# Encoder trunk with grouped experts: expert results read back in eight transfers, all first choices ahead of all second choices

## The chip, the cores and the metric

The kernel runs on one core of a Trainium2 chip. The metric is the device time of one execution in microseconds, the median over several runs. A core has TensorE (PE in the profile), VectorE (DVE), ScalarE (ACT), GpSimd (POOL) and SyncE (SP), which follow their own instruction streams and meet at semaphores, and sixteen DMA engines.

## The reference

Two groups of 256 tokens (512 in all) of width 1024 pass through two encoder layers with shared weights. In float32, a layer is attention in two forms, a gated merge, and then a mixture of experts, in which every token goes to its best two of sixteen experts:

```python
h2 = rms_norm(x, norm_ffn) * (1 + scale2) + shift2
x = x + gate2 * grouped_moe(h2, ...)      # w[t, j]: weight of the token's j-th choice, j = 0, 1
# grouped_moe: out[t] = w[t, 0] * expert_(e[t,0])(h2[t]) + w[t, 1] * expert_(e[t,1])(h2[t])
...
return rms_norm(x, final_norm)            # after layer 2
```

(The reference adds all sixteen experts with a gate that is zero for fourteen of them; the comment gives the sum that is left.) The change lies between the experts' outputs and the `x + gate2 * ...` of both layers.

## The kernel before, in words

All tokens are on the core, in four blocks of 128 (TT = 4). The residual stream is kept transposed in the tensor xT (features on partitions), the experts' rows are not: a tile of 128 token rows is gathered for an expert, goes through its gate, up and down products, and its output rows are scattered by GpSimd to a DRAM tensor y_dram (`y_by_choice`, 1024 rows). Row t of its first half is the output of the first choice of token t, row t of its second half that of the second choice. Tiles are worked in pairs (par 0 and 1); a loop over the pairs, whose length is read from a plan at run time, loads each expert's weights through six ring slots.

When all scatters are stored, the rows are read back to SBUF, into the tensor zone: got[0] for the first choices (4 blocks of 1024 numbers per partition) and got[1] for the second. This is done by load_rows_back (line 675), which SyncE runs at two places.

At the boundary between the layers SyncE has issued the loads of the next layer's first four modulation weight blocks. It then waits for the last scatter (y_stored), issues the readback (line 680), and behind it the loads of the next blocks of the input projection (`qa`, `kva`, `qb`, `kb`; line 673). All go through SyncE's one DMA queue. ScalarE, after copying four modulation rows, does weigh_first (line 1318): for each block it waits for got_rows[t] and scales the first choice by its weight (line 1322). VectorE does combine (line 1851): for each block it waits for ScalarE's count got_weighed and adds the weighted second choice (line 1855). TensorE transposes each block (line 876) to its banks. VectorE then makes the low part of the first weight group (low_part, line 1770), for which ScalarE must have made the high part from the landed block `qa` (line 1316), and only after it adds the gated rows to xT (line 1847). Squares and the norm of the next layer follow.

At the end the order is different. While the rows are on their way, TensorE makes rows of the gates (line 1224) and puts xT, turned back to token rows, into eight banks (line 1232). ScalarE goes through the blocks (lines 1679 to 1686): it weighs block t (line 1681), and from t = 2 on it does the squares and root of block t - 2 (tok_rms, lines 1670 to 1676) after that, so the fourth weighing stands behind the root of block 0. VectorE does gated_sum for blocks 0, 1 and 2: the sum (line 2392) and the product with the gate row (line 2396). Then it scales block 0 by its inverse root (lines 2401 and 2406), does gated_sum for block 3, and scales blocks 1, 2 and 3. TensorE adds each gated block to its banks (line 1238), and SyncE stores each scaled block (line 756).

Before the change a transfer carries both choices of one block (1024 KB, one semaphore got_rows[t]), so whoever waits for the first choice has the second too, and VectorE needs no wait of its own for a DMA.

Of the kernel before, what the change touches and what calls it, by code (L numbers as in the profile page):

```python
# [29 lines left out]
P = 128  # L30
# [4 lines left out]
TOK = SEQ * GROUPS  # L35
TT = TOK // P
DEPTH = 2
# [321 lines left out]
def build_trunk(nc, t_in, y_prompt, y_sample):  # L359
# [7 lines left out]
    with ctx:  # L367
# [3 lines left out]
        def sem(name):  # L371
            return ctx.enter_context(nc.semaphore(name))
# [3 lines left out]
        y_dram = nc.dram_tensor("y_by_choice", (2 * TOK, D), F32, kind="Internal").ap()  # L376
# [24 lines left out]
        def part(at, n):  # L401
            return z[:, at:at + n]
# [31 lines left out]
        got_both = part(0, 8192).rearrange("p (j t d) -> p j t d", j=2, t=TT)  # L434
        got = (part(0, 4096).rearrange("p (t d) -> p t d", t=TT), part(4096, 4096).rearrange("p (t d) -> p t d", t=TT))
# [103 lines left out]
        h2_out = sem("h2_out")  # L539
        index_now = sem("index_now")  # L540
        got_rows = [sem(f"got_rows{t}") for t in range(TT)]
        arrived = sem("arrived")
        go = sem("go")
        planned = sem("planned")
# [106 lines left out]
        def _(sp):  # L651
# [23 lines left out]
            def load_rows_back(pairs, layer):  # L675
                for par in range(2):
                    sp.wait_ge(y_stored[par], pairs * 16 + 16)
                nc.sync.sem_inc(sp_passed, 1)
                for t in range(TT):
                    sp.dma_start(got_both[:, :, t, :],  # L680
                                 y_dram.rearrange("(j t p) d -> p j t d", j=2, p=P)[:, :, t, :])\
                      .then_inc(got_rows[t], 16)

            for t in range(TT):
                x_in = t_in[("x_prompt", "x_sample")[t // 2]]
# [2 lines left out]
            for layer in range(DEPTH):  # L688
# [4 lines left out]
                for b in BLOCKS:  # L693
                    if not TURN[b]:
                        par = 0 if SLOT[b] in EXPERT_SLOTS[0] else 1
                        left = LAST_PARTS[par][EXPERT_SLOTS[par].index(SLOT[b])]
                        sp.wait_ge(part_used, before * 12 + PARTS_BEFORE - left)
                        nc.sync.sem_inc(sp_passed, 1)
                    if b == "qa" and layer:
                        load_rows_back(before, layer)  # L700
                    if TURN[b]:

                        sp.wait_ge(used[SLOT[b]], layer * SLOT_BLOCKS[SLOT[b]] + TURN[b])
                    load(layer, b)
# [44 lines left out]
            nc.sync.sem_inc(sp_passed, 1)  # L749
            sp.dma_start(norm_row, t_in["final_norm"].partition_broadcast(P)).then_inc(in_norm_row, 16)  # L750
            load_rows_back(pairs, DEPTH)

            for t in range(TT):
# [938 lines left out]
        def _(dve):  # L1692
# [73 lines left out]
            def low_part(n):  # L1766

                b, c = W_GROUPS[n]
                dve.wait_ge(S["w_hi_ready"], n + 1)
                v.tensor_tensor(group_view(w_lo[SLOT[b]], b, c), group_view(ring[SLOT[b]], b, c),  # L1770
                                w_hi[:, n % W_BUFS, :, :].bitcast(F32), ALU.subtract).then_inc(S["w_lo_ready"], 1)
# [70 lines left out]
            def add_gated(use, key, j, which):  # L1842

                ps = wait_full(dve, use, key)
                for g in range(GROUPS):
                    x = xT[:, j, g * SEQ:(g + 1) * SEQ]
                    ins = v.scalar_tensor_tensor(x, ps[:, g * SEQ:(g + 1) * SEQ],
                                                 mod[:, 3 * KC * which + 2 * KC + j, g:g + 1], x, ALU.mult, ALU.add)
                freed(ins, use, key)

            def combine(own, use, layer, nth):

                for t in range(TT):
                    dve.wait_ge(S["got_weighed"], nth * TT + t + 1)
                    v.scalar_tensor_tensor(got[0][:, t, :], got[1][:, t, :], gw[:, 1, t:t + 1], got[0][:, t, :],
                                           ALU.mult, ALU.add).then_inc(S["mix_ready"], 1)
                low_part(0)
                for c in range(KC):
                    add_gated(use, ("back", c), c, 1)
                for n in range(1, W_BUFS):  # L1860
                    low_part(n)

            for layer in range(DEPTH):
# [32 lines left out]
                if layer:  # L1896
                    combine(own, use, layer, 0)
                    norm_rstd(own, use, 0)
# [490 lines left out]
            def gated_sum(t):  # L2389

                dve.wait_ge(S["got_weighed"], TT + t + 1)
                own.step(v.scalar_tensor_tensor(got[0][:, t, :], got[1][:, t, :], gw[:, 1, t:t + 1], got[0][:, t, :],
                                                ALU.mult, ALU.add))
                own.last()
                dve.wait_ge(gate_rows_ready, 2 * GROUPS)
                v.tensor_tensor(got[0][:, t, :], got[0][:, t, :], gate_rows[:, t // 2, :], ALU.mult).then_inc(gated, 1)
# [13 lines left out]
            for t in range(3):  # L2410
                gated_sum(t)
            scaled_rows(0)
            gated_sum(3)
            for t in range(1, TT):
                scaled_rows(t)
# [110 lines left out]
```

## Time and profile before

| What | Value |
|---|---|
| Median of 3 runs | 1549.5 us (1547.37 to 1552.57) |
| Profiled execution, its own time | 1550.57 us |
| Its span in the profile | 1548.7 us |
| TensorE busy | 1432.5 us, 92% |
| VectorE busy | 1006.8 us, 65% |
| ScalarE busy | 865.1 us, 56% |
| GpSimd busy | 122.4 us, 8% |
| DMA, mean over the span | 220 GB/s |

The span is the time from the first to the last record. Busy times of different engines lie beside each other and don't add up to it. A DMA's landing is seen from when its semaphore released someone. The readback takes place twice, from 765 us and from 1523 us of the span.

### The profile page before, as it was taken

How to read it: one execution, taken by the hardware profiler on the slowest of the kernel's cores; microseconds unless marked ns; L12 is line 12 of the kernel's file. 1: busy time of each engine (PE TensorE's matmuls, PEld its weight loads, DVE VectorE, ACT ScalarE, POOL GpSimd, SP SyncE). 2: the span in 40 equal slices, each digit the busy share in tenths (PEclk: the TensorE clock that was granted, in tenths of full speed). 3: DMA queues.
4: the chain of work that ended last, by engine and by line, in shares of the span. 5: the costliest groups of instructions: out<-in, count | busy, mean ns of one | idle time of the engine just before them, and what ended most of it. 6: DMA issues, size and time to landing. Idle time of an engine off the chain costs nothing. (4 is left out here: it accounts for less than half of the span.)

```text
span 1548.7 us, 19269 instructions
## 1 busy us (share of the span) xinstructions
PE 1432.5 (92%) x6810; PEld 1088.1 (70%) x6810; DVE 1006.8 (65%) x1256; ACT 865.1 (56%) x1232; POOL 122.4 (8%) x143
## 2 busy tenths in 40 slices
PE   5799989999889999999859999899997999999997
PEld 2677558887667777777537765688774877777775
DVE  1565685325388888888363929733255888888874
ACT  4632595323257777777354228822225577777764
POOL 1000000000021111122000000000000121111110
PEclk8899999999999999999969999999998999999998
DMA  9622761113359999999763138211145599999944
GB/s 325 233 101 104 271 219 55 55 55 109 127 187 353 364 374 357 363 354 361 263 220 109 55 118 321 106 55 55 57 161 194 204 368 369 364 367 361 360 177 167
DMA packets 148368, 341.49 MB, mean 220 GB/s; under 512 B 8351, under 2 KB 10545, under 8 KB 148176
## 3 DMA queue, kind: packets, MB, share of 16 engines
q1 hardware_dynamic: 136880, 317.20, 56.3%
q0 software_dynamic: 10704, 22.57, 4.1%
q10 hardware_dynamic: 720, 0.87, 0.2%
q8 instruction: 39, 0.64, 0.2%
q14 instruction: 25, 0.20, 0.0%
HBM read 333.08 MB, written 24.12 MB: 231 GB/s over the span
## 5 line engine op out<-in xcount | busy, mean ns | idle before, releaser
L778 PE MATMUL bank<-x_hi,w_lo 128*128 128x512 f32 x608 | 244.1, 402 | 19.7 <-DVE w_lo L1770 7.3
L779 PE MATMUL bank<-x_lo,w_hi 128*128 128x512 f32 x608 | 238.8, 393 | 0.0
L780 PE MATMUL bank<-x_hi,w_hi 128*128 128x512 f32 x608 | 238.8, 393 | 0.0
L2278 DVE TENSOR_TENSOR w_lo<-ring,x_lo 128x2048 fp32r<-128x2048 f32 x92 | 210.4, 2289 | 29.0 <-ACT x_lo L1586 28.6
L1586 ACT CAST zone_r<-ring 128x2048 fp32r<-128x2048 f32 x92 | 176.0, 1913 | 28.5 <-PE bank L1155 16.1
L1586 ACT CAST x_lo<-ring 128x2048 fp32r<-128x2048 f32 x92 | 176.1, 1918 | 26.3 <-PE bank L1170 14.6
L1153 PE MATMUL bank<-w_lo,zone_r 128*128 128x512 f32 x384 | 156.0, 406 | 0.0
L1770 DVE TENSOR_TENSOR w_lo<-ring,w_hi 128x1024 fp32r<-128x1024 f32 x84 | 102.2, 1221 | 81.6 <-ACT w_hi L1316 80.9
L778 PEld LDWEIGHTS bank<-x_hi,w_lo 128*128 128x128 f32 x608 | 115.3, 190 | 51.6 <-issue 23.0
L779 PEld LDWEIGHTS bank<-x_lo,w_hi 128*128 128x128 f32 x608 | 115.3, 190 | 26.3 <-issue 2.4
L780 PEld LDWEIGHTS bank<-x_hi,w_hi 128*128 128x128 f32 x608 | 115.1, 189 | 24.6
L1316 ACT CAST w_hi<-ring 128x1024 fp32r<-128x1024 f32 x84 | 87.3, 1046 | 26.7 <-PE bank L780 13.1
L1155 PE MATMUL bank<-zone_r 128*128 128x512 f32 x256 | 101.3, 396 | 0.0
L1154 PE MATMUL bank<-zone_r 128*128 128x512 f32 x256 | 100.9, 394 | 0.0
L1521 ACT ACTIVATE zone<-bank 128x512 f32<-128x512 f32 x32 | 19.1, 598 | 136.1 <-PE bank L780 136.0
L1154 PE MATMUL bank<-x_lo,zone_r 128*128 128x512 f32 x240 | 95.1, 396 | 0.0
L1155 PE MATMUL bank<-x_lo,zone_r 128*128 128x512 f32 x240 | 95.0, 396 | 0.0
L2278 DVE TENSOR_TENSOR w_lo<-ring,zone_r 128x2048 fp32r<-128x2048 f32 x32 | 73.4, 2292 | 21.7 <-ACT zone_r L1586 21.4
L1153 PEld LDWEIGHTS bank<-w_lo,zone_r 128*128 128x128 f32 x384 | 72.3, 188 | 15.5 <-issue 0.2
L2278 DVE TENSOR_TENSOR w_hi<-ring,zone_r 128x2048 fp32r<-128x2048 f32 x32 | 73.4, 2292 | 6.2 <-ACT zone_r L1586 6.0
L2443 POOL DMA_DIRECT2D rows_by_token<-zone x8 | 4.4, 548 | 826.6 <-ACT zone L1569 825.8
L2446 POOL DMA_INDIRECT zone<-rows_by_token,row_now x28 | 53.7, 1917 | 201.3 <-DMA y_by_choice<-zone,row_now 196.1
(316 smaller groups left out, 2766.4 us busy)
## 6 DMA issues: line engine op xcount, KB each, us to landing
ring<-in_w_gate SPq DMA_DIRECT2D x32, 2048.0 KB, 13.7
ring<-in_w_up SPq DMA_DIRECT2D x32, 2048.0 KB, 14.9
ring<-in_w_down SPq DMA_DIRECT2D x32, 2048.0 KB, 9.7
ring<-in_w_ada SPq DMA_DIRECT2D x24, 2048.0 KB, 13.5
ring<-in_w_in SPq DMA_DIRECT2D x16, 2048.0 KB, 7.9
ring<-in_w_out SPq DMA_DIRECT2D x4, 2048.0 KB, 7.7
zone<-y_by_choice SPq DMA_DIRECT2D x8, 1024.0 KB, 8.0
ring<-in_w_branch_a SPq DMA_DIRECT2D x2, 2048.0 KB, 8.3
```

The costliest lines, as they stand in the source:

```text
L778: mm(out, lo, x_first, start=start, stop=False)
L779: mm(out, hi, x_second, start=False, stop=False)
L780: return mm(out, hi, x_first, start=False, stop=stop)
L1153: mm(out, xg_hi[:, par, c, :], wv[:, c, :], start=(c == 0), stop=False)
L1154: mm(out, xg_lo[:, par, c, :], hi[:, k, :], start=False, stop=False)
L1155: ins = mm(out, xg_hi[:, par, c, :], hi[:, k, :], start=False, stop=(c == KC - 1))
L1316: nc.scalar.copy(w_hi[:, n % W_BUFS, :, :], group_view(ring[SLOT[b]], b, c)).then_inc(S["w_hi_ready"], 1)
L1521: af(gates[:, n % 2, :], ps[:, :], ACT.Sigmoid).then_inc(S["gate_ready"], 1)
L1586: nc.scalar.copy(part_hi[buf], ring[EXPERT_SLOTS[par][k]][:, h * 2048:(h + 1) * 2048])\
L1770: v.tensor_tensor(group_view(w_lo[SLOT[b]], b, c), group_view(ring[SLOT[b]], b, c), w_hi[:, n % W_BUFS, :, :].bitcast(F32), ALU.subtract). ...
L2278: v.tensor_tensor(w_low[EXPERT_SLOTS[par][k]][:, cols], ring[EXPERT_SLOTS[par][k]][:, cols], part_hi[buf].bitcast(F32), ALU.subtract)\
L2446: pool.indirect_dma_start(xg[:, par, :], None, h2_dram, bass.IndirectOffsetOnAxis(ap=index, axis=0), bounds_check=TOK - 1, oob_is_err=Fals ...
```

## The change

Each of the four transfers of both choices is replaced by two of 512 KB: SyncE issues the first choices of blocks 0 to 3, then the second choices of blocks 0 to 3. The second choices have four semaphores of their own, got_second, and VectorE waits for them ahead of each sum, at both places.

```diff
--- before.py
+++ after.py
@@ -539,6 +539,7 @@
         h2_out = sem("h2_out")
         index_now = sem("index_now")
         got_rows = [sem(f"got_rows{t}") for t in range(TT)]
+        got_second = [sem(f"got_second{t}") for t in range(TT)]
         arrived = sem("arrived")
         go = sem("go")
         planned = sem("planned")
@@ -677,9 +678,10 @@
                     sp.wait_ge(y_stored[par], pairs * 16 + 16)
                 nc.sync.sem_inc(sp_passed, 1)
                 for t in range(TT):
-                    sp.dma_start(got_both[:, :, t, :],
-                                 y_dram.rearrange("(j t p) d -> p j t d", j=2, p=P)[:, :, t, :])\
-                      .then_inc(got_rows[t], 16)
+                    sp.dma_start(got[0][:, t, :], y_dram[t * P:(t + 1) * P, :]).then_inc(got_rows[t], 16)
+                for t in range(TT):
+                    sp.dma_start(got[1][:, t, :], y_dram[TOK + t * P:TOK + (t + 1) * P, :])\
+                      .then_inc(got_second[t], 16)
 
             for t in range(TT):
                 x_in = t_in[("x_prompt", "x_sample")[t // 2]]
@@ -1852,6 +1854,7 @@
 
                 for t in range(TT):
                     dve.wait_ge(S["got_weighed"], nth * TT + t + 1)
+                    dve.wait_ge(got_second[t], layer * 16)
                     v.scalar_tensor_tensor(got[0][:, t, :], got[1][:, t, :], gw[:, 1, t:t + 1], got[0][:, t, :],
                                            ALU.mult, ALU.add).then_inc(S["mix_ready"], 1)
                 low_part(0)
@@ -2389,6 +2392,7 @@
             def gated_sum(t):
 
                 dve.wait_ge(S["got_weighed"], TT + t + 1)
+                dve.wait_ge(got_second[t], DEPTH * 16)
                 own.step(v.scalar_tensor_tensor(got[0][:, t, :], got[1][:, t, :], gw[:, 1, t:t + 1], got[0][:, t, :],
                                                 ALU.mult, ALU.add))
                 own.last()
```

## Rows read from the trace of the kernel before

**Rows 1.** The page's list of DMA issues (out<-in, engine, operation, count, KB each, median us to landing)

```profile
zone<-y_by_choice SPq DMA_DIRECT2D x8, 1024.0 KB, 8.0
```

**Rows 2.** Source lines 680 (read back) and 756 (store): duration in ns, landing in us

```profile
L680 SPq DMA_DIRECT2D zone<-y_by_choice x8: 372/470/783, 765.4 to 1524.5; - x8
...
L756 SPq DMA_DIRECT2D out<-zone x4: 332/341/351, 1538.2 to 1545.7; - x4
...
DMA to landing us min/median/max: 2.6/2.6/2.7
```

**Rows 3.** Chain of waits, the last 50 us (start us, us, what)

```profile
1523.01 4.78 DMA zone<-y_by_choice
1527.82 1.16 ACT zone L1681
...
1529.08 1.29 DVE zone L2392
1530.40 1.22 DVE zone L2396
1531.62 1.23 DVE zone L2392
...
1539.41 1.24 DVE zone L2396
...
1540.69 2.00 PE bank L1238 x4
```

**Rows 4.** Timeline of the end (start us, us, engine, line, operation; in brackets the idle time before, its releaser)

```profile
1523.01 2.13 SPq L680 DMA_DIRECT2D zone<-y_by_choice  x4
...
1530.37 1.15 ACT L1681 ACTIVATE zone<-zone,gw 128x1024 f32<-128x1024 f32 x1 [1.41 <-DMA zone<-y_by_choice]
...
1531.68 7.11 PE L1238 MATMUL bank<-zone,const 128*128 128x512 f32 x12 [3.19 <-DVE zone L2396]
...
1532.93 1.15 ACT L1681 ACTIVATE zone<-zone,gw 128x1024 f32<-128x1024 f32 x1 [1.41 <-DMA zone<-y_by_choice]
...
1535.98 0.29 ACT L1676 ACTIVATE four<-four 128x1 f32<-128x1 f32 x1
...
1536.58 0.15 DVE L2401 RECIPROCAL four<-four 128x1 f32<-128x1 f32 x1
```

**Rows 5.** Windows (us, each engine's busy us, granted clock PEclk, DMA share, GB/s)

```profile
1509.00:1515.00 6.00, 5.82 (x14) 4.56 (x15) 3.12 (x16) 0.00 (x0) 0.00 (x0) 0.50 0.00 0
...
1529.00:1531.00 2.00, 0.00 (x0) 0.00 (x0) 1.89 (x2) 0.63 (x1) 0.00 (x0) 1.00 1.01 410
1533.00:1534.00 1.00, 1.00 (x3) 0.32 (x1) 1.00 (x1) 1.00 (x2) 0.00 (x0) 0.50 1.01 406
1536.00:1537.00 1.00, 1.00 (x4) 0.47 (x3) 0.96 (x3) 1.00 (x2) 0.00 (x0) 1.00 0.00 0
```

**Rows 6.** Timeline of the boundary between the layers, columns as in rows 4

```profile
765.43 2.23 SPq L680 DMA_DIRECT2D zone<-y_by_choice  x4
...
767.71 16.80 SPq L673 DMA_DIRECT2D ring<-in_w_in  x4
...
773.48 2.48 DVE L1855 SCALAR_TENSOR_TENSOR zone<-zone,gw 128x1024 f32<-128x1024 f32 x2 [0.16 <-DVE mul L1830]
...
779.27 1.15 ACT L1322 ACTIVATE zone<-zone,gw 128x1024 f32<-128x1024 f32 x1 [1.42 <-DMA zone<-y_by_choice]
780.45 1.29 DVE L1855 SCALAR_TENSOR_TENSOR zone<-zone,gw 128x1024 f32<-128x1024 f32 x1 [1.28 <-ACT zone L1322]
781.79 1.97 PE L876 MATMUL bank<-const,zone 128*128 128x128 f32 x8 [1.47 <-DVE zone L1855]
784.78 3.88 ACT L1316 CAST w_hi<-ring 128x1024 fp32r<-128x1024 f32 x4 [4.36 <-DMA ring<-in_w_in]
785.86 1.22 DVE L1770 TENSOR_TENSOR w_lo<-ring,w_hi 128x1024 fp32r<-128x1024 f32 x1 [4.12 <-ACT w_hi L1316]
787.00 6.35 DVE L1847 SCALAR_TENSOR_TENSOR xT<-bank,mod,xT 128x256 f32<-128x256 f32 x16
```

## The prediction, made before the changed kernel was run

> **What bounds the kernel now.** I looked first for the two places where the results are read back, then asked of each what ended its last wait. The page's list of DMA issues [rows 1] shows the eight 1024 KB transfers that the change touches: four at the start of the second layer, four at the end. Everything else stays as it is, so only these two stretches, about 20 us each, can give or lose time.
>
> *The end.* The chain of waits [rows 3] runs: last scatter lands, SyncE issues at 1523.01, the first transfer lands 4.78 us later, ScalarE weighs the first choice from 1527.82, VectorE adds the second choice from 1529.08. From there to 1540.65 the chain is VectorE alone: sum, multiply, sum, multiply, without a gap. Then come the last block's products on TensorE (1540.69), its squares and root on ScalarE, and the last scaling and store. So VectorE's start sets the end, one for one, as long as nothing starves it later.
>
> *The layer boundary.* The timeline [rows 6] shows the same work there, but the four sums end at 780.45 + 1.29 = 781.74, the last transposes at 781.79 + 1.97 = 783.76, and then all engines wait for a weight block: ScalarE's cast at 784.78 was idle for 4.36 us until ring<-in_w_in landed. VectorE's part of that block (785.86) stands ahead of its gated additions (787.00) in program order. The weight block ends the last wait, and the readback has 787.00 - 783.76 = 3.2 us of slack.
>
> **The change part by part.**
>
> *Bytes and their order.* The bytes are the same, 4 MB per place; only the order differs. Before, the transfers land at intervals of one block: ScalarE's waits end at 1527.82, 1530.37 and 1532.93 [rows 3, 4], 2.55 us apart. The windows show 410 GB/s during them [rows 5], and 1.05 MB at 0.41 MB a microsecond is 2.56 us, so they follow one another in order with no gap. A half of the size then takes 1.275 us. The second choice of block 0 is the fifth of eight, two and a half old transfers from the front instead of one. It lands 1.5 x 2.55 = 3.83 us after the old first: 1527.79 + 3.83 = 1531.62.
>
> *ScalarE's weighing.* The weighing of 1.15 us now lies beside the transfers: first choices land near 1526.5, 1527.8, 1529.1 and 1530.3, so block 0 is weighed by 1527.7, and blocks 1 and 2 by 1530.3. ScalarE's fourth weighing stays behind the root of block 0 in program order, and moves with it.
>
> *VectorE's start at the end.* Before 1529.08; after 1531.62 and the 0.05 us that such a handover takes: 1531.67. That is 2.59 us later.
>
> *VectorE afterwards.* The chain has 2.54 us a block (1529.08 to 1531.62 [rows 3]); second choices land every 1.275 us, so blocks 1 to 3 have theirs in time (at 1532.9, 1534.2 and 1535.5, wanted at 1534.2, 1536.8 and 1540.7). VectorE runs without a gap as before, only 2.59 us later. Nothing is handed back: the last block's transfer is not what the old chain waits for.
>
> *The added waits.* Eight waits on VectorE (four a place), whose semaphores are filled for all but the first. Queued behind each are the sum, the multiply, and for TensorE the block's products. The trace has no such wait alone; a sum and the multiply after it, which already has two waits between them, stand 0.03 us apart (1529.08 + 1.29 to 1530.40 [rows 3]). Bounds 0 to 0.05 us each, four at each place; I take 0, nearest to that gap, and keep 0.2 us for the range.
>
> *The issues.* SyncE issues eight in place of four. The old ones take 0.37 to 0.78 us (median 0.47) each, and a 512 KB store takes 0.34 [rows 2]. Eight cost 8 x 0.34 = 2.7 to 8 x 0.53 = 4.2 us against 2.13 [rows 4]. At the end the fifth leaves by 1523.01 + 5 x 0.53 = 1525.7, and its bytes are not wanted before 1530.3: hidden. The first may start moving up to 0.2 us sooner, because its issue is shorter; I take 0 and keep -0.2. At the boundary the queued issues behind them are the weight blocks: the first would leave 2.1 us later than 767.71, near 769.8, while the queue has readback bytes until about 779: hidden. With that cover gone it would cost those 2.1 us.
>
> *The boundary.* The weight block follows the same 4 MB in the same queue, so it lands when it did: 0. First choices are weighed ahead of the sums. The last sum no longer waits for a weighing and can start when the last transfer lands (779.27, where ScalarE's wait for it ends, in place of 780.45), so the transposes end about 1.2 us sooner and wait longer for the same weight block. If that block were not the limit, those 1.2 us would be a gain; VectorE's first sum (773.48) now waits for the fifth half, to 779.25 - 3 x 1.275 = 775.4, and that too stays in the slack, since the sums follow at 1.3 us each and the last starts at 779.3.
>
> *TensorE's clock.* At the end TensorE sits idle for 3.19 us before block 0's products start at 1531.68 [rows 4]; this becomes 5.8 us. The granted clock is 0.50 (the lower level, 1.2 GHz) in the slice at 1533 and 1.00 (2.4 GHz) in that at 1536 [rows 5], so the lower level came within 1.3 us of the restart and was gone 4.3 us after it. After the longer idle time it may already hold at the restart: what ran at the full level, 1.3 us at most, would take as long again. Behind it the root of block 0 comes at 1535.98 + 0.29 = 1536.27 and VectorE asks for it at 1536.58 [rows 4], 0.3 us of cover. Bounds 0 and 1.3 - 0.3 = 1.0 us; I take 0, because the level had fallen early in block 0 as it is, and keep the 1.0. The stretch 1509 to 1515 held 0.50 for 6 us [rows 5]; even that would be over at 1534.3 + 6 = 1540.3, before the last block's products at 1543.3.
>
> *A price for size.* With 410 GB/s and 2.55 us spacing the rows show no fixed cost between transfers of 1 MB. A lone 512 KB store takes 2.6 us from issue to landing [rows 2] against 1.275 of movement, so up to 1.3 us of fixed time per transfer exists and is either hidden by the next or not. The trace has no queue of 512 KB transfers alone. Bounds 0 and 1.3 us each; I take 0, nearest to the spacing row, as the next transfer's bytes are already queued.
>
> The Trainium skill (DMA: Bandwidth & Descriptors, "Anatomy of one DMA" and "Measured") gives each transfer a fixed 2.0 us and advises at least 1 MiB per transfer. The trace agrees for a transfer alone (4.78 less 2.55 is 2.2 us) and not for one in a queue (2.55 us apart); by the page's formula paid in full, each half-size transfer would take 3.2 us, an estimate from that page, and the change would be clearly slower, as in the second rival.
>
> **The sum.** End +2.59, boundary 0, other terms 0: +2.6 us. Against the profiled execution (1550.57 us, span 1548.7) that is 1553.2. This execution stood 1.07 us above the median of 1549.5; the prediction is for medians: 1549.5 + 2.6 = 1552.1 us. That is 0.17% slower, less than the 0.3% (4.6 us) that a measurement of this kernel can tell from no change.
>
> **The rivals.**
>
> *The last landing counts (faster).* If both places are bound by when block 3 is complete, weighing drops out behind it and each gives 1.2 us: 1549.5 - 2.4 = 1547.1. For it: at the boundary ScalarE waited 1.42 us for the last transfer [rows 6]. Against it: the weight block comes later still [rows 6], and VectorE has no gap at the end [rows 3]. Only mixtures of it are likely. Chance 0.06.
>
> *Gaps between the smaller transfers (clearly slower).* Place: the SyncE queue, both places. Each of eight transfers leaves a gap g that its successor doesn't cover. The end pays four gaps before the fifth lands, and the weight block at the boundary stands behind eight and pays 8g (the four before show no gap). Total 2.6 + 4g + 8g. It passes 4.6 us from g = 0.17 us. With g = 0.3 it is 1549.5 + 2.6 + 3.6 = 1555.7; with the full 1.3 it is 1549.5 + 2.6 + 15.6 = 1567.7. Chance 0.12, mostly near the low end.
>
> *Nothing moves.* If the second choices land early, since the sixteen engines drain the queue unevenly, or the first bytes start sooner, VectorE starts where it did: 1549.5. Against it: the landings are evenly spaced. Chance 0.08.
>
> **How the numbers follow.** The forecast has 0.74, with its own range from 2.59 - 0.2 to 2.59 + 0.2 + 1.0, which is 1551.9 to 1553.3, and about 1 us either way for the scatter of a median (the runs shown span 5.2 us): 1551 to 1554. Range for 8 in 10: from 1549.0, which takes in "nothing moves", to 1555.0, which takes in gaps up to 0.24 us. Within 0.3%: most of the forecast, all of "nothing moves" and most of the first rival, 0.77; slower 0.18 (the gaps, and the forecast with unlucky scatter); faster 0.05.
>
> **What would show it.** In the changed kernel: first choices land 1.3 us apart; ScalarE weighs three blocks before VectorE's first sum; that sum follows a DMA, not ScalarE, at about 8.7 us after the first issue (6.07 before); VectorE then has no gap until the last products. At the boundary the cast still waits for the weight block; its distance from the first issue is 784.78 - 765.43 = 19.35 us before [rows 6]. If it grows by more than 0.3 us, the smaller transfers cost something. If VectorE's first sum at the end comes within 7 us of the first issue, the order argument is wrong.

## The result, and the profile after

The changed kernel takes 1555.21 us in the median of 20 runs (1550.61 to 1559.43), the kernel before 1549.26 us in 20 runs (1546.56 to 1556.28). The ratio is 1.0037, with a 95% interval of 1.0025 to 1.0048: about 5.7 us slower (3.9 to 7.4), where 2.6 us were forecast. That is 0.2 us above the upper end of the range, 1555.0, and on the slower side of the 0.3% line, though the interval takes in 0.3%. The ratios of this document leave out two slow executions, of 2383 us (pairs) and 2850 us (before).

| | Before | After |
|---|---|---|
| Profiled execution, its own time | 1550.57 us | 1553.39 us |
| Span | 1548.7 us | 1551.3 us |
| First readback issue at the end, to the end of the span | 1548.7 - 1523.01 = 25.7 us | 1551.3 - 1520.02 = 31.3 us |
| First readback issue at the end, to VectorE's first sum | 6.07 us | 1530.13 - 1520.02 = 10.11 us |
| First readback issue at the boundary, to the cast of the weight block | 19.35 us | 783.25 - 763.77 = 19.48 us |

The two spans alone would mislead: this execution of the changed kernel reached the last readback 3 us earlier than that of before, so the span grew by 2.6 us only. The profiles of all kernels here reach it anywhere from 1519.8 to 1523.0 us. The last stretch shows the loss, 5.6 us, and that agrees with the ratio. A single profile of this stretch can be a microsecond off, though: the kernel boundary_only below, whose end is that of before, has 26.9 us.

The timeline of the end of the changed kernel answers to [rows 3] and [rows 4] (start us, us, engine, line, operation, count; in brackets the idle time before and its releaser):

```profile
1520.02 1.88 SPq L681 DMA_DIRECT2D zone<-y_by_choice  x4
1521.94 1.94 SPq L683 DMA_DIRECT2D zone<-y_by_choice  x4
1523.24 1.15 ACT L1683 ACTIVATE zone<-zone,gw 128x1024 f32<-128x1024 f32 x1 [2.67 <-DMA zone<-y_by_choice]
1525.15 1.15 ACT L1683 ACTIVATE zone<-zone,gw 128x1024 f32<-128x1024 f32 x1 [0.76 <-DMA zone<-y_by_choice]
1527.43 1.15 ACT L1683 ACTIVATE zone<-zone,gw 128x1024 f32<-128x1024 f32 x1 [1.14 <-DMA zone<-y_by_choice]
1530.13 1.28 DVE L2396 SCALAR_TENSOR_TENSOR zone<-zone,gw 128x1024 f32<-128x1024 f32 x1 [20.79 <-DMA zone<-y_by_choice]
1531.45 1.22 DVE L2400 TENSOR_TENSOR zone<-zone,ring 128x1024 f32<-128x1024 f32 x1
1532.59 1.28 DVE L2396 SCALAR_TENSOR_TENSOR zone<-zone,gw 128x1024 f32<-128x1024 f32 x1
1532.72 6.96 PE L1240 MATMUL bank<-zone,const 128*128 128x512 f32 x12 [7.23 <-DVE zone L2400]
...
1538.12 1.41 DVE L2410 SCALAR_TENSOR_TENSOR zone<-bank,four,ring 128x512 f32<-128x512 f32 x2 [0.30 <-DVE four L2405]
...
1539.45 1.27 DVE L2396 SCALAR_TENSOR_TENSOR zone<-zone,gw 128x1024 f32<-128x1024 f32 x1
...
1542.04 3.18 PE L1240 MATMUL bank<-zone,const 128*128 128x512 f32 x4 [2.35 <-DVE zone L2400]
...
1546.83 1.41 DVE L2410 SCALAR_TENSOR_TENSOR zone<-bank,four,ring 128x512 f32<-128x512 f32 x2
```

The 5.6 us come apart here. VectorE's first sum now waits for a DMA, not for ScalarE, and its distance from the first issue has grown by 4.04 us. The fourth sum follows the first by 9.32 us (1538.10 - 1529.08 = 9.02 before): 0.3 us. From the last block's products to the last scaling pass 1546.83 - 1542.04 = 4.79 us, against 1544.28 - 1540.69 = 3.59 before, since the products took 3.18 us and not 1.98: 1.2 us. The rest is 0.05.

The rate of the transfers while they run, for before and then for the changed kernel (slices of 0.35 us from the first issue):

```profile
GB/s 23 0 35 152 117 421 328 433 374 456 421 421 386 456 421 421 386 456 421 421 386 433 433 398 410 386 410 421 421 410 398 386 445 117 0 0 0 0 0 0
```

```profile
GB/s 23 0 59 199 211 398 386 386 421 386 351 199 140 269 304 328 339 375 363 316 351 421 410 421 398 445 421 410 410 445 421 410 410 410 351 176 164 82 0 0
```

Before holds about 415 GB/s from its sixth slice to the end. After falls to 140 GB/s some 4 us in and is back near 415 only at 7.4 us. That is the hole of which the experiments below speak. In these 14 us no queue but SyncE's moves more than one packet (0.01 MB), so it is not another queue's traffic that takes the engines away. The first choices show the hole too: ScalarE's waits for them end 3.2, 5.1 and 7.4 us after the first issue, 1.9 and 2.3 us apart, where 1.3 us apart was forecast.

The boundary, which answers to [rows 6]:

```profile
763.77 1.78 SPq L681 DMA_DIRECT2D zone<-y_by_choice  x4
765.59 1.98 SPq L683 DMA_DIRECT2D zone<-y_by_choice  x4
...
773.98 5.13 DVE L1858 SCALAR_TENSOR_TENSOR zone<-zone,gw 128x1024 f32<-128x1024 f32 x4 [2.32 <-DMA zone<-y_by_choice]
775.31 5.05 PE L878 MATMUL bank<-const,zone 128*128 128x128 f32 x32 [4.44 <-DVE zone L1858]
783.25 3.88 ACT L1318 CAST w_hi<-ring 128x1024 fp32r<-128x1024 f32 x4 [8.76 <-DMA ring<-in_w_in]
```

The transposes end at 775.31 + 5.05 = 780.4, 16.6 us after the first issue (18.3 before), and the cast still waits for the weight block, now with 8.76 us of idle time before it in place of 4.36. Everything that moved lies in that idle time.

### The profile page after: what moved, and what is told of

It reads as the page before. It is cut to its first block and busy times, and to the rows that moved or that the text cites. A ratio compares the mean times of both kernels' runs of the same rounds, so it can differ in the third digit from the quotient of the medians.

```text
span 1551.3 us, 19284 instructions
## 1 busy us (share of the span) xinstructions
PE 1430.7 (92%) x6810; PEld 1087.4 (70%) x6810; DVE 1007.0 (65%) x1256; ACT 865.1 (56%) x1232; POOL 119.7 (8%) x143
## 5 line engine op out<-in xcount | busy, mean ns | idle before, releaser
L2096 DVE TENSOR_TENSOR zone<-bank,zone 128x512 f32<-128x512 f32 x16 | 11.1, 692 | 86.8 <-PE bank L782 86.8
```

## The experiments

Theory at the start: the loss is at the end, and has three parts: the order of the bytes, a hole in the queue that comes with half-size transfers, and TensorE's clock. Each ratio is against executions of the kernel before that were measured beside it. "Above before" is this ratio times 1550 us; the difference of the plain medians departs from it by up to 1.2 us. "First sum" and "last stretch" are in us from the first readback issue of the end, and like the last column they come from one profiled execution each.

| Kernel | Ratio, 95% interval | First sum | Last stretch | Boundary: issue to cast |
|---|---|---|---|---|
| before | 1 | 6.07 | 25.7 | 19.35 |
| changed | 1.0037, 1.0025 to 1.0048 | 10.11 | 31.3 | 19.48 |
| changed_again | 1.0038, 1.0021 to 1.0056 | 10.16 | 30.4 | 20.87 |
| end_only | 1.0023, 1.0009 to 1.0038 | 9.32 | 29.3 | 19.37 |
| boundary_only | 1.0004, 0.9993 to 1.0014 | 6.34 | 26.9 | 20.27 |
| pairs | 1.0007, 0.9995 to 1.0020 | 5.00 | 26.0 | 19.87 |
| megabyte | 1.0035, 1.0022 to 1.0048 | 10.43 | 31.6 | 19.54 |
| one_early | 1.0015, 1.0003 to 1.0026 | 5.79 | 28.3 | 19.69 |
| mixed | 1.0022, 1.0009 to 1.0035 | 9.04 | 29.7 | 19.42 |
| fill | 1.0030, 1.0018 to 1.0043 | 10.18 | 30.5 | 19.48 |
| before_fill | 1.0002, 0.9988 to 1.0016 | 6.07 | 25.7 | 19.33 |
| pairs_fill | 0.9995, 0.9982 to 1.0008 | 5.69 | 27.5 | 19.99 |

**end_only.** The new transfers and VectorE's new wait at the end only:

```diff
-                for t in range(TT):
-                    sp.dma_start(got_both[:, :, t, :], ...).then_inc(got_rows[t], 16)
+                if layer == DEPTH:
+                    ...  # the eight transfers of the changed kernel
+                else:
+                    ...  # the four of before
```

> Eight transfers, first choices first, at the end alone; at the layer boundary the four old transfers of both choices. In the profiles of before and after, the stretch from the first readback issue of the end to the end of the span went from 1548.7 - 1523.01 = 25.7 us to 1551.3 - 1520.02 = 31.3 us, 5.6 us more, and the boundary's stretch from first issue to the cast of the weight block from 19.35 to 19.48 us. Theory (the end holds the whole loss): this kernel is as slow as the changed one, 5 to 6 us above before, ratio 1.0032 to 1.0038, and its last stretch takes 30 to 31.5 us. Rival (gaps between smaller transfers at both places): about 2 to 4 us above before, since the boundary's share is missing.

Measured: 1.0023, 3.5 us above before (1.4 to 5.9); last stretch 29.3 us, just under the 30 to 31.5 forecast. The time lies in the rival's range of 2 to 4 us and not in the theory's 5 to 6, but its interval reaches into both. So the end holds most of the loss; that it holds all of it is not shown. In this profile the hole was small (its lowest slice has 269 GB/s, first sum at 9.32 us, not 10.1).

**boundary_only.** The same with the condition the other way round, and VectorE's new wait only there:

```diff
-                if layer == DEPTH:
+                if layer < DEPTH:
```

> The eight transfers at the layer boundary alone; at the end the four old ones. Theory (the boundary waits for the weight block anyway): the time of before within 1 us, ratio 0.9993 to 1.0007; the cast of the first weight block starts 19.3 to 19.6 us after the first readback issue. Rival (gaps): 2 to 4 us slower, the cast more than 20.5 us after the first issue.

Measured: 1.0004, no loss that can be told (-1.1 to 2.2 us). But the cast came 20.27 us after the first issue, 0.9 us later, between the two expectations. In the seven profiles with eight half-size transfers at the boundary the distance is 19.48, 20.87, 20.27, 19.87, 19.69, 19.48 and 19.99, mean 19.95; in those with four transfers it is 19.33 to 19.37 (19.54 in megabyte). So the weight block lands 0.6 us later on average, and the sums play no part in it. The dip differs between executions: in slices of 0.5 us, the lowest rate between 4 and 5 us after the first issue is 172 GB/s in boundary_only, 254 in changed_again, 295 in changed and 328 in fill, with the cast at 20.27, 20.87, 19.48 and 19.48 us. Whether the 0.6 us reach the end is not shown: from the first issue at the boundary to the first issue at the end, the profiles with the four old transfers at the boundary take 755.7 to 757.6 us, those with eight 754.8 to 757.6.

**pairs.** All eight transfers, in the order of blocks:

```diff
                 for t in range(TT):
                     sp.dma_start(got[0][:, t, :], y_dram[t * P:(t + 1) * P, :]).then_inc(got_rows[t], 16)
-                for t in range(TT):
                     sp.dma_start(got[1][:, t, :], y_dram[TOK + t * P:TOK + (t + 1) * P, :])\
```

> The same eight 512 KB transfers, semaphores and waits as the changed kernel at both places, but in the order first choice of block 0, second choice of block 0, first of block 1, and so on. Theory A (the order alone makes the loss): VectorE's first sum comes 1.2 us sooner than before (6.07 us after the first issue before, 4.9 here), since the weighing lies beside the second transfer, and the kernel is 0 to 1.2 us faster than before. Theory B (half-size transfers also leave holes in the queue; the profile after shows 184 GB/s in the slice 4 us after the first issue, and the second choice of block 0 landed 10.0 us after it and not 8.6): the first sum comes at 5 to 6.5 us, and later sums wait for transfers; within 1.5 us of before, on either side.

Measured: 1.0007, 1.1 us above before, which can't be told from equal (-0.8 to 3.1 us). With the same sizes, number and waits as the changed kernel most of the 5.7 us are gone, and the two intervals lie apart; so the order makes most of the loss. What theory B says of the holes also shows:

```profile
1527.95 1.28 DVE L2395 SCALAR_TENSOR_TENSOR zone<-zone,gw 128x1024 f32<-128x1024 f32 x1 [14.70 <-DMA zone<-y_by_choice]
1529.27 1.23 DVE L2399 TENSOR_TENSOR zone<-zone,ring 128x1024 f32<-128x1024 f32 x1
1530.24 1.15 ACT L1682 ACTIVATE zone<-zone,gw 128x1024 f32<-128x1024 f32 x1 [2.81 <-DMA zone<-y_by_choice]
...
1531.69 1.28 DVE L2395 SCALAR_TENSOR_TENSOR zone<-zone,gw 128x1024 f32<-128x1024 f32 x1 [1.19 <-DMA zone<-y_by_choice]
```

These are VectorE's first two sums, with the issue at 1522.95. The first comes at 5.00 us, 1.07 earlier than before. The second waits 1.19 us for a transfer and comes at 8.74 us (8.55 in the timeline of before): what hiding the weighing won was lost again while transfers ran behind their even pace, down to 234 GB/s in one slice.

**megabyte.** Choice by choice in four transfers of 1024 KB:

```diff
+                for t in range(0, TT, 2):
+                    sp.dma_start(got[0][:, t:t + 2, :], y_dram[t * P:(t + 2) * P, :].rearrange("(t p) d -> p t d", p=P))\
+                      .then_inc(got_rows[t], 16)
+                ...  # the same for got[1]; waits on got_rows and got_second of block t // 2 * 2
```

> Choice by choice, but in four transfers of 1024 KB: first choices of blocks 0 and 1, first choices of blocks 2 and 3, then the second choices likewise. The second choice of block 0 is complete with the third transfer. If only bytes and order count: it lands 4.78 + 2 x 2.55 = 9.9 us after the first issue, as late as the 10.0 us of the changed kernel, and the kernel is as slow as the changed one, 5 to 6 us above before. If reading whole choices (rows that lie one after another) is itself slower than reading both choices alternately, it lands at 11 us or later and the kernel is 7 us or more above before. If the holes belong to the half size, the landings are evenly 2.5 to 2.6 us apart, as in before.

Measured: 1.0035 in five executions, 5.4 us above before and as slow as the changed kernel, with no hole. Its rates from the first issue:

```profile
GB/s 23 0 59 70 12 152 363 421 398 410 456 410 410 410 456 410 410 410 456 410 410 386 433 421 421 398 375 433 433 410 398 386 410 421 129 0 0 0 0 0
```

The first landing ends ScalarE's wait 0.4 us later than in before (after 5.19 us, not 4.81), and the third transfer is complete after 10.4 us in place of 9.9. That it is as slow as the changed kernel is a balance of two things: here 3 MB must land ahead of the first sum and there is no hole, in the changed kernel 2.5 MB and the hole. So order by choice alone costs about 5 us when the transfers are this large, the clock's share included (the last block's products took 3.26 us here). Reading whole choices runs at 410 GB/s like before, no slower in itself.

**one_early.** The second choice of block 0 moved from fifth place to second:

```diff
+                for j, t in [(0, 0), (1, 0), (0, 1), (0, 2), (0, 3), (1, 1), (1, 2), (1, 3)]:
+                    sp.dma_start(got[j][:, t, :], ...).then_inc((got_rows, got_second)[j][t], 16)
```

> The changed kernel with one transfer moved, at both places: the second choice of block 0 goes second instead of fifth; all else, sizes and waits, as changed. Theory (VectorE's last wait for a second choice sets the end): VectorE sums block 0 at 5.0 us after the first issue and then waits for the second choice of block 1, now the sixth transfer, which lands at 4.78 - 1.28 + 5 x 1.275 = 9.9 us, or up to 1.4 us later with a hole in the queue; in before that block's sum started at 8.6. So 1.3 to 2.7 us above before from the transfers, with TensorE's clock 1.3 to 4 us, against 5.6 for the changed kernel. Rival (eight transfers cost their time by number and size, not by order): as slow as the changed kernel, 5 us or more above before.

Measured: 1.0015, 2.3 us above before (0.5 to 4.0). The issue is at 1520.28:

```profile
1526.07 1.28 DVE L2394 SCALAR_TENSOR_TENSOR zone<-zone,gw 128x1024 f32<-128x1024 f32 x1 [15.25 <-DMA zone<-y_by_choice]
...
1531.49 1.28 DVE L2394 SCALAR_TENSOR_TENSOR zone<-zone,gw 128x1024 f32<-128x1024 f32 x1 [2.88 <-DMA zone<-y_by_choice]
```

VectorE waits 2.88 us for block 1, whose sum comes at 11.21 us, 2.7 later than before; the last stretch is 2.6 us longer too (28.3). The loss follows the last second choice that VectorE waits for: one transfer moved, and more than half of it is gone.

**fill.** TensorE turns three blocks of xT back twice at the end; the first result is overwritten:

```diff
+            for t in range(3):
+                for half in range(2):
+                    ps = take(final_use, ("x_tok", t, half))
+                    for q in range(4):
+                        mm(ps[:, q * P:(q + 1) * P], xT[:, 4 * half + q, t * P:(t + 1) * P], K("ident"),
+                           start=(q == 0), stop=(q == 3))
```

> The changed kernel with TensorE given 24 more groups of identity products at the end (three of the four blocks of xT are turned back twice, the first result overwritten), so that it sits idle for about 1.7 us and not 7.2 us before block 0's products. No other engine's work changes and the result is the same. Theory (part of the end's loss is TensorE's clock, which drops to the lower level in the longer idle stretch: the last block's four products took 3.18 us in place of 1.98, and VectorE waited 0.3 us twice): the clock stays at 1.00 through the end, the last block's products take 2.0 us, and the kernel is 1.0 to 1.8 us faster than the changed one in the same call, 3.5 to 4.5 us above before. Rival (the clock falls anyway or isn't waited for): equal to the changed kernel within 0.5 us.

Measured: 1554.35 us against 1555.06 for changed_again beside it, 0.7 us by the medians and 1.2 us by the ratios (1.0030 and 1.0038): at the lower edge of the theory or between the two expectations, and not resolved, since the intervals overlap. Products of the four blocks in the timeline of fill:

```profile
1535.01 1.98 PE L1246 MATMUL bank<-zone,const 128*128 128x512 f32 x4 [1.94 <-DVE zone L2406]
...
1537.46 1.98 PE L1246 MATMUL bank<-zone,const 128*128 128x512 f32 x4 [0.47 <-DVE zone L2406]
...
1539.92 1.98 PE L1246 MATMUL bank<-zone,const 128*128 128x512 f32 x4 [0.47 <-DVE zone L2406]
...
1543.89 2.73 PE L1246 MATMUL bank<-zone,const 128*128 128x512 f32 x4 [1.99 <-DVE zone L2406]
```

The filling did what it should for blocks 0 to 2: full speed, and VectorE never waits for a root but the last. The last block, after 1.99 us of idle time, still met the lower level in this execution, against the expectation. So the clock costs time in two places: after the long idle time before block 0, which filling cures, and after the short one before the last block, which it left as it was.

**changed_again.** No edit; the changed kernel measured again, beside fill, one_early and before_fill.

> The changed kernel once more, to be compared in the same call: 5 to 6 us above before, ratio 1.003 to 1.004; VectorE's first sum at the end 9.3 to 10.2 us after the first readback issue; the last stretch from that issue to the end of the span 30 to 31.5 us.

Measured as expected, 1.0038. In this execution the last block's products took 1.98 us, in the first profile 3.18:

```profile
1534.86 7.94 PE L1240 MATMUL bank<-zone,const 128*128 128x512 f32 x12 [7.27 <-DVE zone L2400]
...
1544.42 1.98 PE L1240 MATMUL bank<-zone,const 128*128 128x512 f32 x4 [1.63 <-DVE zone L2400]
```

The same kernel pays the last 1.2 us in one execution and not in another. Here the first three blocks ran longer at the lower level (7.94 us, not 6.96), VectorE waited 0.34 and 0.30 us at block 0's root, and TensorE then sat idle for 1.63 us and not 2.35 before the last block. The fourth sum followed the first by 9.57 us, so the clock cost 0.6 us in this execution and 1.5 in the first.

**before_fill.** The same filling with one block, in the kernel before:

```diff
+            for t in range(1):
+                ...  # as in fill
```

> The kernel before with TensorE given 8 more groups of identity products at the end (one block turned back twice), so that its idle time of 3.2 us before block 0's products becomes 1.4 us. Theory: in before, VectorE's chain covers most of what the lower clock costs, so this gains little, 0 to 0.7 us; the granted clock stays at 1.00 in all of the end. Rival (before loses to the clock as the changed kernel does): 1.0 us or more faster than before.

Measured: 1.0002, nothing gained, as expected; the products ran at 1.98 us in all four blocks and the last stretch stayed at 25.7 us.

**mixed.** First choices in two transfers of 1024 KB, second choices in four of 512 KB:

```diff
-                for t in range(TT):
-                    sp.dma_start(got[0][:, t, :], y_dram[t * P:(t + 1) * P, :]).then_inc(got_rows[t], 16)
+                for t in range(0, TT, 2):
+                    sp.dma_start(got[0][:, t:t + 2, :], y_dram[t * P:(t + 2) * P, :].rearrange("(t p) d -> p t d", p=P))\
+                      .then_inc(got_rows[t], 16)
                 ...  # second choices as in the changed kernel
```

> Choice by choice, the first choices in two transfers of 1024 KB (blocks 0 and 1, blocks 2 and 3), the second choices in four of 512 KB. So far every kernel with eight 512 KB transfers showed a stretch below 300 GB/s at the third to fifth microsecond, and none with 1024 KB transfers did. If the holes come from half-size transfers at the head of the queue, they are absent here, the second choice of block 0 lands 4.78 + 2.55 + 1.275 = 8.6 to 9.1 us after the first issue, as the prediction had it, and the kernel is 2.5 to 4 us above before, between it and the changed kernel. If the holes come from reading whole choices, or come wherever 512 KB transfers follow, it lands at 10 us as in the changed kernel, and the kernel is 4.5 to 6 us above before.

Measured: 1.0022, 3.4 us above before (1.4 to 5.4). The first sum comes at 9.04 us, with the issue at 1519.83, and there is no hole:

```profile
1528.87 1.28 DVE L2397 SCALAR_TENSOR_TENSOR zone<-zone,gw 128x1024 f32<-128x1024 f32 x1 [19.66 <-DMA zone<-y_by_choice]
```

```profile
GB/s 23 0 59 129 47 281 293 456 386 445 398 456 363 445 421 433 398 445 410 445 375 421 445 398 421 374 421 421 410 433 375 398 433 258 94 0 0 0 0 0
```

This is the change as the prediction had computed it, and its first sum comes 1.1 us sooner than the changed kernel's. (By time alone the two kernels' intervals overlap.) In these profiles holes come when half-size transfers stand at the head of the queue, not when they follow larger ones. All seven profiles with eight half-size transfers at the end dip below 300 GB/s in the middle of the queue there (to between 140 and 269), and none of the five whose queue begins with 1024 KB does once it is up to speed. Why the engines stand idle there stays open.

**pairs_fill.** The order of pairs, with one block filled on TensorE:

```diff
+            for t in range(1):
+                ...  # as in fill, added to pairs
```

> Eight 512 KB transfers block by block (first choice, second choice), and TensorE given one block of products twice at the end. In the same order without the added products, VectorE started 1.1 us sooner than before and lost it again waiting for block 1. If that loss is the holes alone, this is equal to before within 1 us, and TensorE's clock stays at 1.00. If TensorE's clock took a part of it, this is 0.5 to 1.2 us faster than before.

Measured: 0.9995, level with before, and 1.2 permille under pairs with overlapping intervals. VectorE waited 0.36 us for block 1 and not 1.19, but it had started 0.7 us later than in pairs (first sum at 5.69 us); block 1's sum came at 8.60 us, as in before. The clock did not stay up: after 1.99 us of idle time the last block's products took 3.68 us. It beats the changed kernel, and can't be told from the old one.

## Why the prediction was right in part and wrong in part

- *VectorE's start sets the end, one for one.* Right, apart from the clock. In the changed kernel VectorE never waits for a transfer after its first sum; pairs and one_early moved the wait, and the time followed.
- *The order costs 1.5 transfers, 2.59 us.* Right in kind and near in size. Mixed, where the second choice of block 0 has the same bytes ahead of it and the queue no hole, put the first sum 2.97 us later than before. 0.3 of that is a later first landing (it ends ScalarE's wait after 5.08 us, not 4.81), which leaves 2.7.
- *"A price for size ... I take 0, nearest to the spacing row."* This step failed. The spacing row was one of 1024 KB transfers, and the half-size ones leave a hole: 10.11 - 8.66 = 1.4 us at the end, and the weight block at the boundary about 0.6 us late. Nearly all of it lies ahead of the third landing, which ends ScalarE's wait 7.4 us after the first issue where 6.1 was forecast; from there to VectorE's first sum it is 2.7 us for two transfers, near the forecast 2.55. The rival with gaps had this mechanism, with the wrong shape: not a gap a transfer, four then eight, but one dip near the head of the queue, so the boundary did not pay twice what the end pays. That this rival's 1555.7 us (for a gap of 0.3) lies so near the measured 1555.2 is luck: 2.4 of its 3.6 us stood at the boundary.
- *TensorE's clock: "I take 0".* Mis-sized. The profile after shows 0.3 us through block 0's root and 1.2 us in the last block, that of changed_again 0.6 and 0. I had argued that the lower level would be over before the last block; it was over (1.00 from 1536 on), stayed at 1.00 through the 2.35 us of idle time, and fell again some 0.7 us after the last block's products had started. That second fall was not in my account. Fill, which takes away the first part only, gained 0.7 us by the medians against changed_again, not resolved.
- *The boundary: 0.* Right for the sums, the transposes and SyncE's issues, which all vanish in the wait for the weight block; wrong by 0.6 us on average for the weight block itself, which stands behind the hole. No run shows that these 0.6 us lengthen the whole.
- *The added waits and issues: 0.* Right. Sum and multiply stand 0.04 us apart as before, and the eight issues are out 3.9 us after the first, before the second transfer has landed.
- *The 2.0 us per transfer.* The section of the Trainium skill that the prediction names (DMA: Bandwidth & Descriptors, "Anatomy of one DMA") fits this figure to transfers that GpSimd issues, and the prediction left that out; these are issued by SyncE. At the estimated 3.2 us each, eight would take 25.6 us. The changed kernel's are through 13.3 us after the first issue, against 11.9 us for the four before, so little of such a fixed cost is left over per transfer in this queue.
- The sum with the sizes from the profiles: 2.6 (order) + 1.4 (hole at the end) + 0 to 0.6 (hole at the boundary) + 0.6 to 1.5 (clock) is 4.6 to 6.1 us, against 5.7 measured (3.9 to 7.4). The first term is shown by runs (pairs, one_early); the hole and the clock are read from profiles, and no difference of times resolves either.

The changed kernel's wait, seen as one view: granted clock and rate in slices of the end (us, busy us of PE, PEld, DVE, ACT, POOL, PEclk, DMA share, GB/s).

```profile
1524.00:1525.00 1.00, 1.00 (x12) 1.00 (x11) 0.00 (x0) 0.39 (x1) 0.00 (x0) 1.00 0.53 184
...
1529.00:1530.00 1.00, 0.00 (x0) 0.00 (x0) 0.00 (x0) 0.00 (x0) 0.00 (x0) 0.52 1.01 414
...
1536.00:1537.00 1.00, 1.00 (x4) 0.43 (x3) 0.97 (x2) 0.69 (x2) 0.00 (x0) 1.00 0.00 0
...
1541.00:1542.00 1.00, 0.00 (x0) 0.00 (x0) 1.00 (x2) 0.93 (x5) 0.00 (x0) 1.00 0.68 270
1542.00:1545.00 3.00, 2.96 (x4) 0.85 (x4) 2.93 (x6) 0.97 (x3) 0.00 (x0) 0.61 0.22 87
```

The first line is the hole, DMA engines busy for 0.53 of the slice with eight transfers issued. In the second none of these engines works at all: three of the first choices are weighed and the first second choice is still under way. The third and fourth show the clock back at the higher level, and still there while TensorE is idle; the last shows it fallen again during the last block's products (in finer slices it is 1.00 from 1542.0 to 1542.5 and 0.50 from 1543.0 on).

## What to carry to other kernels

When a consumer needs two inputs per block, the order of the transfers should be the order in which blocks become complete: putting all first inputs ahead moved the end of the first complete block from the second of eight half transfers to the fifth, and a consumer that is the bottleneck from then on never makes it up. Splitting a transfer so that part of the work can lie beside it is a separate step from reordering; here the split in block order gained 1.1 us at the first sum and had lost it by the second. A spacing measured for one size of transfer does not price another size, even where the queue is full: here the half size lost 1.4 us at the end. And a loss of 6 us in 1550 is read from the distances inside the profile; most differences of times here could not tell the parts apart.

## What the runs showed that was not expected

A queue that begins with 512 KB transfers dipped, in the changed kernel to 140 to 300 GB/s for about a microsecond around its third transfer, although its first four had all been issued 1.9 us after the first issue, some 2 us ahead of the dip; with 1024 KB at its head it held about 415 GB/s. The depth differs between executions (lowest slice of the end 140 to 269 GB/s), and its cause stays open.

The granted clock of TensorE fell during the last block's four products in six of the twelve profiles and stayed up in the other six. It fell after 1.99 (fill, pairs_fill), 2.09, 2.10, 2.32 and 2.35 us of idle time, and the products took 2.73, 3.68, 2.68, 2.41, 3.26 and 3.18 us. It stayed up after 0.77 to 1.90 us in four profiles and after 1.99 us in two (pairs, before_fill), and the products took 1.98 us. So the same idle time of 1.99 us went either way.
